# Hybrid decoder step on one core: last squares taken channel-major, the root moved into the logits, first expert rows gathered in float32, the opening table in four parts, softmax limits head by head

## The reference, cut to what matters

```
h = rmsnorm(x, norm_mix);  xr, q, k, v, g_rnn, g_attn = split(h @ w_in)      # 1024 x 4352
y_rnn  = rg_lru(causal_conv(xr, 4 taps), gates from w_rg, w_ig)               # a scan over tokens
y_attn = window_attend(q, k, v)           # 16 heads, window 128, ALiBi, sink in the softmax
x = x + [sigmoid(g_rnn) * y_rnn, sigmoid(g_attn) * y_attn] @ w_out            # 2048 x 1024
t = rmsnorm(x, norm_ffn);  logits = t @ w_router + b_router                   # 32 experts
top_v, top_i = top_k(logits, 4);  wts = softmax(top_v)
for the rows of each expert e:                                                # w_up 1024 x 2048, w_down 1024 x 1024
    z = t @ w_up[e] + b_up[e];  y = min(glu, 7) * sigmoid(1.702 glu) * (clip(lin, -7, 7) + 1)
    x += wts * (y @ w_down[e] + b_down[e])
y = rmsnorm(x, norm_final)
```

## Time and profile before

| | us |
|---|---|
| median of 3 runs | 1142.85 (1142.77 to 1142.86) |
| the profiled execution | 1141.49 |
| its span, first to last instruction | 1139.7 |
| PE busy / DVE / ACT / POOL | 1107.2 / 311.6 / 228.7 / 34.5 |
| DMA | 437.90 MB, 384 GB/s over the span, 428 in most slices |
| mean granted TensorE clock | 0.999 of full speed |

### The profile page before, as it was taken

One profiled execution on the slowest core, in us unless ns is written; L12 is line 12 of the kernel. 1 busy time (PEld: TensorE's weight loads), 2 busy tenths in 40 slices (PEclk: granted clock), 3 DMA queues, 4 the chain that ended last, 5 costly groups with the idle time before them and its releaser, 6 DMA issues.

```text
span 1139.7 us, 14908 instructions
## 1 busy us (share of the span) xinstructions
PE 1107.2 (97%) x5771; PEld 491.4 (43%) x5772; DVE 311.6 (27%) x790; ACT 228.7 (20%) x639; POOL 34.5 (3%) x71
## 2 busy tenths in 40 slices
PE   9999999999999999999999999999999999999997
PEld 6787878744343333333333333333232323232422
DVE  6565562122212121213031212121212120312123
ACT  3663544412020101010111111111111111010103
POOL 1200012200000000000000000000000000000000
PEclk9999999999999999999999999999999999999999
DMA  9843528999999999999999999999999999999995
GB/s 351 306 148 119 169 92 339 408 369 422 428 426 427 427 430 425 429 427 430 427 429 430 426 431 427 430 427 429 430 426 430 428 429 428 428 428 426 428 425 238
DMA packets 40651, 437.90 MB, mean 384 GB/s; under 512 B 6689, under 2 KB 9017, under 8 KB 10921
## 3 DMA queue, kind: packets, MB, share of 16 engines
q1 hardware_dynamic: 39984, 435.65, 91.7%
q10 hardware_dynamic: 624, 1.68, 0.4%
HBM read 436.00 MB, written 2.41 MB: 385 GB/s over the span
## 4 chain that ended last, share of the span: by engine, by line
PE 69%; DMA 24%; DVE 3%; ACT 2%; issue 1%; DVEq 0%; SPq 0%
PE bank L1339 22%; DMA ring<-in_w_down 20%; PE bank L1375 19%; PE bank L1074 8%; PE bank L1120 5%; PE bank L1221 4%; DMA area<-in_w_down 3%; PE bank L1242 3%; PE bank L1170 2%; PE bank L1255 1%; PE bank L1218 1%; PE bank L1245 1%; DVE area L1781 1%; PE bank L956 1%; PE bank L1056 1%
## 5 line engine op out<-in xcount | busy, mean ns | idle before, releaser
L1339 PE MATMUL bank<-ring,area 128*64 128x512 f32 x1744 | 396.4, 597 | 8.8 <-DMA ring<-in_w_up 8.6
L1339 PEld LDWEIGHTS bank<-ring,area 128*64 128x64 f32 x1744 | 117.1, 136 | 261.5 <-issue 225.3
L1375 PE MATMUL bank<-ring,area 128*64 128x512 f32 x928 | 213.8, 599 | 7.5 <-DMA ring<-in_w_down 7.5
L1769 DVE TENSOR_TENSOR x_tok<-x_tok,bank 128x512 f32<-128x512 f32 x60 | 41.3, 688 | 328.0 <-PE bank L1242 328.0
L824 ACT ACTIVATE area<-area 128x256 f32<-128x256 f32 x64 | 26.7, 417 | 515.7 <-DVE area L1781 515.7
L1074 PE MATMUL bank<-ring 128*128 128x264 f32 (+1 forms) x512 | 119.6, 391 | 0.0
L1375 PEld LDWEIGHTS bank<-ring,area 128*64 128x64 f32 x928 | 62.4, 136 | 117.9 <-issue 102.7
L1074 PEld LDWEIGHTS bank<-ring 128*128 128x128 f32 x512 | 95.8, 190 | 20.0 <-issue 1.3
L1806 DVE TENSOR_TENSOR area<-area 128x1024 f32<-128x1024 f32 x15 | 18.4, 1226 | 211.2 <-ACT area L834 211.2
L1242 PE MATMUL bank<-area 128*128 128x512 f32 x128 | 71.8, 644 | 0.0
L1339 PE MATMUL bank<-area 128*64 128x512 f32 x304 | 69.2, 597 | 1.1 <-DMA area<-in_w_up 1.1
(11 more groups left out here) (269 smaller groups left out, 693.5 us busy)
## 6 DMA issues: line engine op xcount, KB each, us to landing
ring<-in_w_up SPq DMA_DIRECT2D x103, 2048.0 KB, 33.4
ring<-in_w_down SPq DMA_DIRECT2D x51, 2048.0 KB, 33.1
area<-in_w_up SPq DMA_DIRECT2D x17, 2048.0 KB, 28.9
ring<-in_w_in SPq DMA_DIRECT2D x16, 1024.0 KB, 9.3
ring<-in_w_down SPq DMA_DIRECT2D x13, 1024.0 KB, 10.0
ring<-in_w_up SPq DMA_DIRECT2D x12, 1024.0 KB, 8.9
area<-in_w_down SPq DMA_DIRECT2D x5, 2048.0 KB, 33.4
ring<-in_w_out SPq DMA_DIRECT2D x8, 1024.0 KB, 5.0
```

The source lines that it names most:

```text
L1339: m = mm(bank[2 * h + n][64 * e:64 * e + 64, :], xe[:, k, 64 * e:64 * e + 64], w[:, kk, e, NB * n:NB * (n + 1)], start=False, stop=(k == K ...
L1375: m = mm(bank[4 + c][64 * e:64 * e + 64, :], y_t[:, 4 * half + f, 64 * e:64 * e + 64], w[:, f, e, :], start=False, stop=(half == 1 and f = ...
L1769: eng.tensor_tensor(x, x, combined_bank(unit, last)[:, :], ALU.add).then_inc(s.added, 1)
```

## The change

It does seven things.

1. The opening table comes in four parts (k = 0, 1, 2-3, 4-7). The identity table `keep` is requested by ACT after its last opening work, not after its first. `norm_sum()` moves from before block n = 1's last product to inside block n = 2, behind its third; the wait for `keep` moves to the transposes that use it. PE opens with 36 narrow fillers where there were five wide and 16 narrow ones.
2. Softmax limits: the limit of a pair's first head is taken before the second head's second maximum, and each head's probabilities are scaled as soon as its own sum is there.
3. The copy of the sixth head pair's output (jj = 6) is made one trunk block earlier.
4. The last block's squares are taken channel-major, from x before it is transposed, and summed over channels by three small matmuls; the other blocks' sums enter by a matmul with the identity. The last block's logits are made token-major directly; those of the first seven blocks are turned before the last block is there.
5. The logits are not divided by the root. Instead the bias is multiplied by it, and the reciprocal goes into the exponent's scale.
6. Pair 0's one-hot matrices are written in float32, times the row's reciprocal root, in six pieces; its rows are gathered from float32 x by three float32 matmuls a block. The separate gather of the root for pair 0 is gone.
7. Of the twelve wide fillers at the router three are left.

```diff
-            ends = (0, *(KB + k * (COLS + T) for k in (1, 2, 4, 6, KB)))
+            ends = (0, *(KB + k * (COLS + T) for k in (1, 2, 4, KB)))
...
@@ ScalarE
             x_scale(1)
-            eng.dma_start(keep[:, :], c_in[:, 0:C_KEEP]).then_inc(s.consts_loaded, 16)
...
             x_scale(5)
-            eng.wait_ge(s.open_loaded4, 16)
+            x_scale(7)
             act(sq[:, KB - 2:KB, :], x_raw[:, KB - 2:KB, :], ACT.Square).then_inc(s.sq_done, 1)
-            x_scale(7)
+            eng.dma_start(keep[:, :], c_in[:, 0:C_KEEP]).then_inc(s.consts_loaded, 16)
...
-                if st >= 6 and st % 2 == 0 and st <= 2 * KB + 2:
-                    for jj in range((st - 6) // 2, (st - 4) // 2 if st < 2 * KB + 2 else KB):
-                        eng.wait_ge(s.pv_done, jj + 1)
-                        act(m_t[:, KB + jj, 0:2 * P], bank[5][:, 0:2 * P], ACT.Copy).then_inc(s.pv_evac, 1)
+                if st >= 6 and st % 2 == 0 and st <= 2 * KB + 2 or st == 2 * KB + 1:
+                    jj = (st - 6) // 2 if st <= 2 * KB else st - 2 * KB + 5
+                    eng.wait_ge(s.pv_done, jj + 1)
+                    act(m_t[:, KB + jj, 0:2 * P], bank[5][:, 0:2 * P], ACT.Copy).then_inc(s.pv_evac, 1)
...
+                if m == KB - 1:
+                    eng.wait_ge(s.x2_ready, 3 * m + 1)
+                    act(last_sq, x_res[:, m, 0:2 * P].rearrange("p (t c) -> p t c", t=2), ACT.Square).then_inc(s.squares, 1)
+                    eng.wait_ge(s.logits_done, 4)
+                    act(stat[:, 6:9], sum_cols, ACT.Sqrt, bias=eps[:, :], scale=1.0 / D).then_inc(s.root, 1)
@@ TensorE
+                    if n == 2 and k == 3:
+                        norm_sum()
...
+            def last_logits():
+                m = KB - 1
...
+                    eng.wait_ge(s.x2_ready, 3 * m + (2 if t == 2 else 1))
+                    own = x_res[:, m, P * t:P * (t + 1)] if t < 2 else xt[:, m % 2, 0:TRIO]
+                    ml = mm(lg_bank[t][0:n, :], own, wr[:, m, :], start=False, stop=True, skip_group_check=True)
...
+            def last_sums():
+                eng.wait_ge(s.squares, SQUARES)
...
+                    m = mm(sum_cols[0:n, t:t + 1], last_sq[:, t, :] if t < 2 else tail_sq[:, 0:TRIO],
+                           ones_col, start=False, stop=(t == 2), skip_group_check=True)
...
+            def first_tile(j, t):
...
+                rows = x_tok[r, t, P * j:P * (j + 1)] if t < 2 else x_tail[r, P * (j % 4):P * (j % 4 + 1)]
+                m = mm(first_bank(j)[:, P * (j % 4):P * (j % 4 + 1)], rows, gw[r, t, :], start=(t == 0), stop=(t == 2))
...
-                    keep_warm(4, bank[5])
-                    slot_rows(q, 5)
-                    first_rows(0)
-                    first_rows(1)
+                    for t in range(3):
+                        eng.wait_ge(s.oh_tile, t + 1)
+                        for j in range(2):
+                            first_tile(j, t)
@@ VectorE
+            for t in range(3):
+                for e in range(2):
+                    ins = eng.scalar_tensor_tensor(out=gw[:, t, CAP * e:CAP * (e + 1)], in0=iota[:, 0:CAP],
+                                                   scalar=rank_m[:, t, e:e + 1],
+                                                   in1=stat[:, 9 + t:10 + t].to_broadcast([P, CAP]),
+                                                   op0=ALU.is_equal, op1=ALU.mult)
+                ins.then_inc(s.oh_tile, 1)
```

More of the change, by code:

```diff
@@ L775, in exponentials @@
                     eng.wait_ge(s.negtop, 1)
-                    act(ex[0:n, t, :], lg[0:n, t, 0:E_N], ACT.Exp, bias=ntop[0:n, t:t + 1]).then_inc(s.top_exp, 1)
+                    act(ex[0:n, t, :], lg[0:n, t, 0:E_N], ACT.Exp, bias=ntop[0:n, t:t + 1],
+                        scale=stat[0:n, 9 + t:10 + t]).then_inc(s.top_exp, 1)
             eng.wait_ge(s.zeroed, 9)
@@ L788, in _ @@
                 act(x_tok[:, :, cols], both, ACT.Copy)
-                if m == KB - 1:
-                    eng.wait_ge(s.sumsq, 1)
-                    act(stat[:, 6:9], stat[:, 0:3], ACT.Sqrt, bias=eps[:, :], scale=1.0 / D).then_inc(s.root, 1)
                 act(parts[:, :, 0, cols], both, ACT.Copy).then_inc(s.split_copy, 1)
@@ L1174, in _ @@
                 out_block(m)
-            keep_warm(2, bank[0])
+            logit_rows(0, 3)
+            eng.wait_ge(s.sumsq, 1)
+            mm(sum_cols, ident, stat[:, 0:3], start=True, stop=False, skip_group_check=True)
+            last_logits()
+            last_sums()
             token_rows(KB - 1)
-            logits(KB - 1, KB)
-            logit_rows()
-            keep_warm(6, bank[0])
             eng.wait_ge(s.tables_ready, 3)
             eng.wait_ge(s.bias_step, 5)
-            eng.wait_ge(s.split_copy, 6 * (KB - 1) + 2)
-            biases(0, 4, 0)
+            keep_warm(3, bank[0])
+            biases(0, 3, 0)
             eng.wait_ge(s.selb_ready, 1)
@@ L1578, in attention_sum @@
                     eng.reciprocal(sm[:, col + 6:col + 8], sm[:, col + 4:col + 6]).then_inc(s.rden, 1)
-                for p in range(2):
-                    buf, col = probs[:, 2 * (j % 2) + p, :], 16 * (j % 2) + 8 * p
+                    buf = probs[:, 2 * (j % 2) + p, :]
                     eng.wait_ge(s.rden, 2 * j + p + 1)
@@ L1725, in _ @@
+            height = (P, P, TRIO)
+            eng.wait_ge(s.root, 2)
+            eng.wait_ge(s.logits_done, 3)
+            for t, n in enumerate(height):
+                ins = eng.scalar_tensor_tensor(out=lg[0:n, t, 0:E_N], in0=br[0:n, :], scalar=stat[0:n, 6 + t:7 + t],
+                                               in1=lg_bank[t][0:n, :], op0=ALU.mult, op1=ALU.add)
+            eng.reciprocal(stat[:, 9:12], stat[:, 6:9]).then_inc(s.rstd_ready, 1)
             router_step(ins)
             for t, n in enumerate(height):
-                ins = eng.max(top[0:n, t, :], lg[0:n, t, 0:E_N])
+                ins = eng.max(top[0:n, t, 0:8], lg[0:n, t, 0:E_N])
@@ L1736, in _ @@
[L1736 to L1740 removed]
+            eng.wait_ge(s.rstd_ready, 1)
+            eng.scalar_tensor_tensor(out=ntop[:, 0:3], in0=top[:, :, 0], scalar=-1.0, in1=stat[:, 9:12], op0=ALU.mult,
+                                     op1=ALU.mult).then_inc(s.negtop, 1)
@@ new lines, in _ @@
+            ranks = bank[4][:, 0:3 * E_N].rearrange("p (t e) -> p t e", t=3)
+            eng.wait_ge(s.selb_ready, 1)
+            eng.wait_ge(s.rank_done, 1)
+            router_step(eng.scalar_tensor_tensor(out=rank_m[:, :, 0:2], in0=ranks[:, :, 0:2], scalar=1.0,
+                                                 in1=selb[:, :, 0:2], op0=ALU.add, op1=ALU.mult))
+            for t in range(3):
+                for e in range(2):
[4 more added lines that the diff above has]
+                ins.then_inc(s.oh_tile, 1)
@@ L1834, in _ @@
             eng.memset(gw_t[:, NT:2 * P + 64], 0.0)
+            gather_hots(0, 0, first)
             weight_hots(0, 0)
```

169 lines of the change are left out of this document (89 added, 80 removed).

## The result

The changed kernel takes **1146.0 us** (median of 7 runs, 1145.1 to 1147.1) against 1142.85 us on the same chip; the ratio is 1.0031 (95% interval 1.0021 to 1.0040), so it is 3.5 us (2.4 to 4.6) slower. The forecast was 1144.6 us and "no change".

The account below looks back on a forecast made before the run. The stream of DMA loads was taken to set the end. Opening +2.3, softmax -0.43, last `pv` -0.85, router -0.4 and gathers +1.1 gave +1.7 on 1142.85, so 1144.6 us, range 1141.3 to 1146.2 us.

Parts of the forecast that it names:

- Opening: Opening: the later channel sum makes TensorE wait for DVE's conv before gate 1, +2.3 us (+1.9 to +2.9).
- The last part's 2.6 us behind part 3: Opening table: k = 4 to 7, 1.1 MB in one part, come in 2.6 us at the full rate; 9.9 us taken.
- Rival B: The opening costs nothing, as the convs catch up or the part lands at 8 us: 1142.3 us; chance 0.22.
- Softmax and last `pv`: Trunk: TensorE's idle time goes at the first softmax, -0.43 us, and before the last `pv`, -0.85 us.
- Router: From the last trunk block to the first expert product: -0.4 us, between -2.0 and +0.5.
- the first product: Pair 0's first expert product, whose time T sets the loads' restart: forecast at 232.2 us against 231.60 before.
- Gathers: Pair 0: two blocks' float32 gathers take 1.68 instead of 0.89 us, three times; +1.1 us lost (0 to +2.4).
- The slack of 1.3 us: Pair 0's loads: the DMA engines have 1.3 us of slack, subtracted from TensorE's 2.4 us of lateness.
- Rival D: TensorE's clock falls at the router with fewer fillers, a load taking 7.2 instead of 3.6 us: 1148.2 us; chance 0.08.

Follow-up runs that it names:

- e9: Kernel before with the change's opening alone, its own fillers kept: 2.4 us above before (1.4 to 3.4).
- e10: Kernel before with only the change's softmax limits by head and earlier copy of the sixth pair's result: 1140.98 us, 1.6 us under before.
- e11: Changed kernel without the eight decode rows' products in the gathers of blocks 2 to 7, plus 12 narrow fillers: 1.5 us above before (0.5 to 2.5).
- e2: Changed kernel with blocks 2 to 7 of pair 0 gathered in three bfloat16 parts as before: 0.6 us above before (-0.5 to 1.6).
- e5: Changed kernel with the opening of before, its 36 narrow fillers kept: 2.2 us above before (1.1 to 3.2).
- e8: Changed kernel with before's opening, 36 narrow fillers kept, and bfloat16 gathers for blocks 2 to 7: 1141.35 us, 1.5 us under before.
- e15: Kernel before with four fillers behind each of pair 0's three gathers, 8 of 16 narrow opening fillers removed: 2.1 us above before (1.0 to 3.1).
- e16: Changed kernel with pair 0's six float32 products for two blocks reordered, the eight-row ones last: 2.5 us above before (1.4 to 3.5).
- e17: Changed kernel with before's opening and pair 0's float32 products reordered, the eight-row ones last: 0.5 us above before (-0.6 to 1.5).
- e1: Changed kernel with the opening and its fillers as before, loop beginning at instruction 3772: 8.2 us above before (6.6 to 9.8).
- e4: Kernel before with six fillers behind each of pair 0's three gathers, loop beginning at instruction 3834: 9.7 us above before (8.1 to 11.3).
- e6: Kernel before with six fillers behind each of pair 0's three gathers, 12 of 16 narrow opening fillers removed: 3.2 us above before (1.9 to 4.6).
- e7: Kernel before with 13 of its 16 narrow opening fillers removed, loop beginning at instruction 3772: 1148.89 us, 5.9 us above before.
- e13: Kernel before with two fillers behind each of pair 0's three gathers: 0.8 us above before (-0.2 to 1.8).

## Why the prediction was wrong

Point by point, forecast against trace:

- **Opening, +2.3 us**: right. 2.2 us between the middles of the twelve and seven traces; alone (e9) it costs 2.4 us. The last part's 2.6 us behind part 3 was right too; that it came at 10.30 instead of 9.9 us is part 3's later landing in that execution. Rival B, that it costs nothing, fell.
- **Softmax and last `pv`, -1.28**: right in kind, 1.55 in every trace. Alone (e10) -1.6 us.
- **Router, -0.4**: -0.84 in every trace, twice the forecast and inside its bounds.
- So the first product was forecast 0.6 us late and was 0.2 late.
- **Gathers, +1.1**: this is the step that failed, and by its size. Its working, "so 0.28 each, 1.68 us", took six equal products from a row in which all have 128 rows. The four of that kind cost 0.27 us each (e11), the two of eight rows between them 0.51 each. With 2.11 us the pitch is 5.70, and the term's own formula gives 3 x (5.70 - 4.90) = +2.4 us instead of +1.1. Undone, the gathers are worth 2.2 us in bytes (changed less e2) and 2.3 (e5 less e8), and 3.0 and 3.7 us in the medians. The slack of 1.3 us, the shakier-looking number, was about right: 3 x (4.90 - 4.48) = 1.26, or 1.0 with the bend at the estimated 4.8. After the first trace I took it for the faulty one, since the windows looked as if nothing had been hidden; e15, e16, e17 and the bytes took that back.
- **Rival D, 0.08**: its mechanism is there, in about a third of executions of such kernels, at some 2 us each in e11 rather than 3.6. Leaving out the two runs under 0.998 moves the changed kernel's median by 0.8 us; with the 1147.1 us run among the rest, that is a hint and not a measurement.

With the gathers put right: 0.2 + 2.4 = 2.6 us. The changed kernel's five runs at the higher mean clock lie 1145.2 - 1142.85 = 2.3 us above before, all seven 3.5 (2.4 to 4.6), and the bytes say 3.1. So between nothing and 0.9 us is left over; low-clock executions may be it, which is not shown.

The forecast "no change" was wrong although 1146.0 us lies inside its range of 1141.3 to 1146.2: the middle lay 1.7 us up, near the bound of 2.3, and the price of an unseen shape was extrapolated at one value with the range kept on the slack. The prediction's own bounds add up to 1143.1 to 1146.5 us, not to the 1142.9 to 1146.0 that it gives the forecast.

## What to carry to other kernels

Where a stream of loads sets the end, turn every TensorE delay into the pitch at which places come free and compare it with the time of a load at full rate: what stays under it is free, what exceeds it is paid at each load. Price a matmul by a row of its own height and its own neighbours, and put products of equal height together. Before a difference of two traces is read as the price of an edit, see how far the first landing moves between executions: here it was 0.5 us of the 2.7. And when an experiment is several microseconds off every theory, look at the instruction queue and at the loop's turns before explaining it by the edit.

## What the runs showed of the hardware

- **A loop's place in TensorE's code costs 6 us here.** With 1768 instructions it is free when it begins at 3798 to 3814, and costs about 3 us of standing at each of three turns, and half the clock behind each, when it begins at 3772 or 3834. 27 more packets of 16.4 KB (0.90 MB in 55 against 0.46 in 28) in three turns are nine at each. Undone by padding, it was worth 6.0 us between e1 and e5 and 6.5 between e4 and e6. The Trainium skill, in "Runtime: NRT & Kernel Launch", section "Instruction fetch mechanics", says that code comes in blocks of 16 KB or 256 instructions, that TensorE holds 2048 of them, and that a taken branch out of the current window of two pages waits for its target. The trace agrees on the size of the blocks and on the wait, but a jump back over 1768 instructions was free in 28 packets, so what is held is more than two blocks. As an estimate from its 256, 1768 instructions fill seven blocks only if they begin within 24 of a block's start. This fits both sides of what was seen if a block starts between 3790 and 3798 in this count, which no run shows; eight blocks, which its 2048 would allow, would hold the loop wherever it began, and at 3772 and 3834 it was not held.
- **Eight-row float32 products between 128-row ones cost 0.51 us against 0.27** (2.11 us interleaved, 1.09 without the two of eight rows), and 0.32 when they stand together (1.73).
- **Half a microsecond of landing at the start is still there 220 us later.** In six traces with before's opening, trunk and router (before, e4, e6, e7, e13, e15) the sum over channels starts at 12.89 to 13.63 us, as the opening's parts land, and the first expert product at 231.60 to 232.31 us, 218.7 us behind it in each.
